# Compact 64x64 tiles in the second mixer's triangular inverse, and normalisation per half of the tokens

## What is computed

```python
def rmsnorm(x, g):
    xf = x.astype(jnp.float32)
    y = xf * lax.rsqrt(jnp.mean(xf * xf, axis=-1, keepdims=True) + EPS)
    return (y * g.astype(jnp.float32)).astype(x.dtype)
```

```python
    def step(S, inp):
        r_t, k_t, v_t, d_t, kk_t, a_t = inp
        S = (S * d_t[:, :, None, :]
             - jnp.einsum('bhvk,bhk->bhv', S, kk_t)[..., None] * (kk_t * a_t)[:, :, None, :]
             + v_t[..., None] * k_t[:, :, None, :])
        return S, jnp.einsum('bhvk,bhk->bhv', S, r_t)
```

## Time and profile before

| | us |
|---|---|
| median of three runs (range) | 2458.49 (2456.34 to 2458.69) |
| the profiled execution | 2457.47 |
| its span, first to last instruction | 2455.7 |
| PE busy in the span | 2189.4 (89%) |
| DVE busy | 656.2 (27%) |
| ACT busy | 355.1 (14%) |
| POOL busy | 136.7 (6%) |

### The profile page before, as it was taken

One profiled execution on the slowest core, in us unless ns is written; L12 is line 12 of the kernel. 1 busy time (PEld: TensorE's weight loads), 2 busy tenths in 40 slices (PEclk: granted clock), 3 DMA queues, 4 the chain that ended last, 5 costly groups with the idle time before them and its releaser, 6 DMA issues. The chain is left out here.

```text
span 2455.7 us, 32351 instructions
## 1 busy us (share of the span) xinstructions
PE 2189.4 (89%) x13312; PEld 1917.6 (78%) x13312; DVE 656.2 (27%) x1048; ACT 355.1 (14%) x658; POOL 136.7 (6%) x136
## 2 busy tenths in 40 slices
PE   6997889877899999999899867939999999999687
PEld 5876777746788888887688645739999999999676
DVE  4286332353200000003531376131001100000033
ACT  1552111110000000001222111010111100111011
POOL 0011111141000000000000200010000000000100
PEclk9998877878999999999999866959999999999888
DMA  7211000011122222212222210028777778877520
GB/s 302 69 52 43 1 1 1 1 35 48 60 78 77 69 79 93 72 65 67 87 73 77 75 52 20 18 77 290 238 258 254 254 250 284 269 239 250 212 81 35
DMA packets 70963, 282.78 MB, mean 115 GB/s; under 512 B 7952, under 2 KB 9104, under 8 KB 69600
## 3 DMA queue, kind: packets, MB, share of 16 engines
q1 hardware_dynamic: 63680, 255.53, 31.3%
q0 software_dynamic: 5040, 19.02, 2.0%
q10 hardware_dynamic: 2160, 7.03, 0.8%
HBM read 255.46 MB, written 26.10 MB: 115 GB/s over the span
## 5 line engine op out<-in xcount | busy, mean ns | idle before, releaser
L189 PE MATMUL ps<-normed,ring 128*128 128x260 f32 (+1 forms) x3424 | 764.1, 385 | 16.7 <-DVE normed L232 16.7
L189 PEld LDWEIGHTS ps<-normed,ring 128*128 128x128 f32 (+1 forms) x3424 | 652.4, 191 | 125.6 <-issue 22.9
L2140 PE MATMUL ps<-proj,ring 128*128 128x144 f32 x3168 | 392.7, 287 | 5.3 <-issue 4.8
L2140 PEld LDWEIGHTS ps<-proj,ring 128*128 128x128 f32 x3168 | 390.8, 191 | 7.6 <-issue 7.0
L2150 PE MATMUL ps<-wide,ring 128*128 128x144 f32 x1584 | 210.9, 293 | 0.0
L2150 PEld LDWEIGHTS ps<-wide,ring 128*128 128x128 f32 x1584 | 205.2, 196 | 0.9
L189 PE MATMUL ps<-proj,ring 128*128 128x260 f32 x640 | 151.8, 399 | 18.3 <-PEq L877 8.4
L189 PEld LDWEIGHTS ps<-proj,ring 128*128 128x128 f32 x640 | 127.2, 200 | 41.0 <-issue 14.0
L189 PE MATMUL ps<-wide,ring 128*128 128x260 f32 x704 | 154.6, 383 | 0.9 <-DVE wide L1176 0.9
L189 PEld LDWEIGHTS ps<-wide,ring 128*128 128x128 f32 x704 | 133.7, 190 | 21.8 <-DVE wide L1176 1.3
L2216 DVE TENSOR_TENSOR wide<-temps,ps 128x144 f32<-128x144 f32 x99 | 30.1, 304 | 369.7 <-PE ps L2140 369.7
(11 more groups left out here) (441 smaller groups left out, 1860.0 us busy)
## 6 DMA issues: line engine op xcount, KB each, us to landing
ring<-in_w_moe_gu SPq DMA_DIRECT2D x198, 512.0 KB, 4.3
ring<-in_w_moe_dn SPq DMA_DIRECT2D x72, 704.0 KB, 5.7
ring<-in_w_gu SPq DMA_DIRECT2D x44, 512.0 KB, 3.6
ring<-in_w_in_cd SPq DMA_DIRECT2D x25, 512.0 KB, 3.5
ring<-in_w_in_ab SPq DMA_DIRECT2D x22, 512.0 KB, 3.6
ring<-in_w_dn SPq DMA_DIRECT2D x16, 704.0 KB, 4.1
ring<-in_w_ple SPq DMA_DIRECT2D x16, 640.0 KB, 3.9
slots_hbm<-wide POOLq DMA_DIRECT2D x1, 9216.0 KB, 30.1
```

The source lines that it names most:

```text
L189: mm = pe.matmul(dst[0:width, a:a + HALF], slab[:, k * width:(k + 1) * width], x[:, a:a + HALF], start=first and k == 0, stop=last and k = ...
L2140: mm = pe.matmul(hid_psum(m, s), slot(Q_MOE + 2 * m + s)[:, f * P:(f + 1) * P], XG(f), start=f == 0, stop=f == KD - 1)
```

## The change

The head pairs are stored compactly: AL, DD, EE, GG, OO become 128x512 (8 tiles of 64 columns, head 0 on the upper, head 1 on the lower partitions), and each 128x128 product of the loop becomes two 64x64 products, one for each head, on its own quarter of PE's array (`hs`, `hp`). PSUM halves are 256 columns (`hp4`). EE starts from a second set of products, with the operands of ab exchanged, masked with `upper`, in place of the transposes L704 and the ACT copy L782. The masks shrink from 961 to 641 columns; a POOL memset of the block-diagonal tiles falls away. In the normalisation, `norm_dve` does reciprocal and scaling first for columns 0 to 259, then for 260 to 519; the first slab does all eight k for the first half and then all eight for the second (`first_product`); the router waits again before its third token group; the output's stores wait for the second half of their tiles.

```diff
@@ -226,18 +226,22 @@
 
         def norm_dve(dve, gain):
             dve.wait_ge(norm_root.sem, norm_root.at(1))
-            dve_step.on(dve.reciprocal(RINV, ROOT))
-            dve.wait_ge(dve_step.sem, dve_step.count)
-            for k in range(KD):
-                u_ready.on(dve.scalar_tensor_tensor(out=u3[:, k, :], in0=h3[:, k, :], scalar=v(gain, k), in1=RINV,
-                                                    op0=ALU.mult, op1=ALU.mult))
-
-        def normed(pe):
-
-            def tile(k):
-                pe.wait_ge(u_ready.sem, u_ready.at(k + 1))
-                return u3[:, k, :]
-            return tile
+            for a in (0, HALF):
+                half = slice(a, a + HALF)
+                dve_step.on(dve.reciprocal(RINV[:, half], ROOT[:, half]))
+                dve.wait_ge(dve_step.sem, dve_step.count)
+                for k in range(KD):
+                    u_ready.on(dve.scalar_tensor_tensor(out=u3[:, k, half], in0=h3[:, k, half], scalar=v(gain, k),
+                                                        in1=RINV[:, half], op0=ALU.mult, op1=ALU.mult))
+
+        def first_product(pe, dst, slab, width=P):
+
+            for n, a in enumerate((0, HALF)):
+                for k in range(KD):
+                    pe.wait_ge(u_ready.sem, u_ready.at(KD * n + k + 1))
+                    mm = pe.matmul(dst[0:width, a:a + HALF], slab[:, k * width:(k + 1) * width],
+                                   u3[:, k, a:a + HALF], start=k == 0, stop=k == KD - 1)
+            return mm
...
-        rwmask, level = Dm[:, 0:P], lambda l: Dm[:, P * (1 + l):P * (2 + l)]
-        sign, i64 = Dm[:, 7 * P:7 * P + 1], Dm[:, 7 * P + 1:7 * P + 65]
+        rwmask, level = Dm[:, 0:P], lambda l: Dm[:, P + 64 * l:P + 64 * (l + 1)]
+        upper, sign, i64 = Dm[:, 512:576], Dm[:, 576:577], Dm[:, 577:641]
         pairs = lambda ap: ap.rearrange("p (n c) -> p n c", c=P)
-        AL, DD, EE, GG = [pairs(u_sb[:, n * 1024:(n + 1) * 1024]) for n in range(4)]
-        OO = pairs(C[:, 0:1024])
+        heads = lambda ap: ap.rearrange("p (n c) -> p n c", c=64)
+        AL, DD, EE, GG, EO = [heads(u_sb[:, n * 512:(n + 1) * 512]) for n in range(5)]
+        OO = heads(C[:, 0:512])
...
+        def hp(bank, hh, n):
+
+            j = 512 * (n // 4) + 64 * (n % 4)
+            return ps[bank][64 * hh:64 * hh + 64, j:j + 64]
+
+        def hs(tile, hh, n):
+
+            return tile[64 * hh:64 * hh + 64, n, :]
+
+        def hp4(bank, cc):
+
+            return heads(ps[bank][:, 512 * cc:512 * cc + 256])
...
-                    for cc in range(2):
-                        for t in range(4):
-                            n = (4 * cc + t) * P
-                            for hh in range(2):
-                                mm = pe.matmul(ps[0][64 * hh:64 * hh + 64, n + 64 * hh:n + 64 * hh + 64],
-                                               rk(t, 2 * s + cc, RKAP, hh), rk(t, 2 * s + cc, RB, hh),
-                                               start=True, stop=True)
-                    g["ab_mm"].on(mm)
+                    for first, second, at in ((RKAP, RB, 0), (RB, RKAP, 512)):
+                        for cc in range(2):
+                            for t in range(4):
+                                n = at + 64 * (4 * cc + t)
+                                for hh in range(2):
+                                    mm = pe.matmul(ps[0][64 * hh:64 * hh + 64, n:n + 64], rk(t, 2 * s + cc, first, hh),
+                                                   rk(t, 2 * s + cc, second, hh), start=True, stop=True)
+                        g["ab_mm"].on(mm)
...
-                    w(pe, "d_ready", s + 1)
                     w(pe, "am_read", 2 * s + 2)
-                    for n in range(8):
-                        mm = pe.transpose(ps[1][:, n * P:(n + 1) * P], DD[:, n, :], ident)
-                    g["e_mm"].on(mm)
                     w(pe, "v_read", s + 1)
                     for l in range(5):
                         for cc in range(2):
                             if l == 0:
-                                w(pe, "o_ready", 2 * s + cc + 1)
-                                w(pe, "e_read", s + 1)
+                                w(pe, "o_ready", s + 1)
                             else:
                                 w(pe, "next_o", 8 * s + 2 * (l - 1) + cc + 1)
                                 w(pe, "de_read", nth(s, l - 1, cc))
                             for n in range(4 * cc, 4 * cc + 4):
-                                mm = pe.matmul(ps[0][:, n * P:(n + 1) * P], OO[:, n, :], EE[:, n, :], start=True, stop=True)
+                                for hh in range(2):
+                                    mm = pe.matmul(hp(0, hh, n), hs(OO, hh, n), hs(EE, hh, n), start=True, stop=True)
                             g["g_mm"].on(mm)
                         for cc in range(2):
                             w(pe, "g_read", nth(s, l, cc))
                             for n in range(4 * cc, 4 * cc + 4):
-                                if l < 4:
-                                    pe.matmul(ps[1][:, n * P:(n + 1) * P], GG[:, n, :], DD[:, n, :], start=True, stop=True)
-                                mm = pe.matmul(ps[2][:, n * P:(n + 1) * P], DD[:, n, :], GG[:, n, :], start=True, stop=True)
+                                for hh in range(2):
+                                    if l < 4:
+                                        pe.matmul(hp(1, hh, n), hs(GG, hh, n), hs(DD, hh, n), start=True, stop=True)
+                                    mm = pe.matmul(hp(2, hh, n), hs(DD, hh, n), hs(GG, hh, n), start=True, stop=True)
                             g["eg_mm"].on(mm)
...
-                    w(act, "e_mm", s + 1)
-                    g["e_read"].on(act.activation(u_sb[:, 2048:3072], ps[1][:, :], ACT.Copy))
...
-                            g["g_read"].on(act.activation(u_sb[:, 3072 + 512 * cc:3584 + 512 * cc],
-                                                          ps[0][:, 512 * cc:512 * cc + 512], ACT.Copy))
+                            g["g_read"].on(act.activation(GG[:, 4 * cc:4 * cc + 4], hp4(0, cc), ACT.Copy))
...
-                    w(dve, "ab_mm", s + 1)
-                    for hh in range(2):
-                        j = 64 * hh
-                        S(dve.tensor_copy(AL[j:j + 64, :, j:j + 64], pairs(ps[0][j:j + 64, :])[:, :, j:j + 64]),
-                          g["ab_read"] if hh else None)
+                    w(dve, "ab_mm", 2 * s + 1)
+                    S(dve.tensor_copy(AL, heads(ps[0][:, 0:512])))
+                    w(dve, "ab_mm", 2 * s + 2)
+                    S(dve.tensor_copy(EO, heads(ps[0][:, 512:1024])), g["ab_read"])
                     S(dve.tensor_tensor(OO, AL, spread(level(0), 8, 1), ALU.mult))
-                    S(dve.tensor_tensor(DD, spread(ident, 8, 1), OO, ALU.subtract), g["d_ready"])
-                    for cc in range(2):
-                        n = slice(4 * cc, 4 * cc + 4)
-                        S(dve.tensor_tensor(OO[:, n], AL[:, n], spread(level(1), 4, 1), ALU.mult), g["o_ready"])
+                    S(dve.tensor_tensor(DD, spread(i64, 8, 1), OO, ALU.subtract))
+                    S(dve.tensor_tensor(EO, EO, spread(upper, 8, 1), ALU.mult))
+                    S(dve.tensor_tensor(EE, spread(i64, 8, 1), EO, ALU.subtract))
+                    S(dve.tensor_tensor(OO, AL, spread(level(1), 8, 1), ALU.mult), g["o_ready"])
...
-                            n, half = slice(4 * cc, 4 * cc + 4), slice(512 * cc, 512 * cc + 512)
+                            n = slice(4 * cc, 4 * cc + 4)
                             w(dve, "eg_mm", nth(s, l, cc))
                             if l < 4:
-                                S(dve.tensor_tensor(DD[:, n], DD[:, n], pairs(ps[1][:, half]), ALU.subtract))
-                            S(dve.tensor_tensor(EE[:, n], EE[:, n], pairs(ps[2][:, half]), ALU.subtract), g["de_read"])
+                                S(dve.tensor_tensor(DD[:, n], DD[:, n], hp4(1, cc), ALU.subtract))
+                            S(dve.tensor_tensor(EE[:, n], EE[:, n], hp4(2, cc), ALU.subtract), g["de_read"])
...
@@ -1127,8 +1137,11 @@
...
-                            product(pe, pt(2 * (m % 2) + s), slot(Q_GU + 2 * m + s), KD,
-                                    normed(pe) if m == 0 and s == 0 else lambda n: u3[:, n, :]).then_inc(slab_used.sem, 1)
+                            if m == 0 and s == 0:
+                                mm = first_product(pe, pt(0), slot(Q_GU))
+                            else:
+                                mm = product(pe, pt(2 * (m % 2) + s), slot(Q_GU + 2 * m + s), KD, lambda n: u3[:, n, :])
+                            mm.then_inc(slab_used.sem, 1)
...
@@ -1936,8 +1949,8 @@
...
-                        if tt == 0:
-                            pe.wait_ge(u_ready.sem, u_ready.at(k + 1))
+                        if tt in (0, 2):
+                            pe.wait_ge(u_ready.sem, u_ready.at(KD * (tt // 2) + k + 1))
...
@@ -2259,7 +2272,7 @@
...
```

(22 more changed lines are left out.)

3 lines of the change are left out of this document (1 added, 2 removed).

## The result

| | us |
|---|---|
| before, median of the runs beside it | 2458.59 |
| after, median of four runs (range) | 2386.84 (2383.67 to 2390.46) |
| ratio, 95% interval | 0.9709 (0.9691 to 0.9727) |
| the profiled execution after, its span | 2388.85, 2387.0 |

The gain is 71.8 us; the forecast had 56.3, and 2386.8 lies just under the lower end of its range, 2388. The direction and the mechanism held, sizes did not. Where the 15.5 us came from is the question of what follows.

A forecast was written before the change was run, and what follows sets the result against it. Bound: a single chain through PE, with DVE's subtractions limiting between loop levels. Loops 43.9, heads 9.9, chain -2 and normalisation 4.5 make 56.3 us less: 2402 us; range 2390 to 2418, 8 in 10 within 2388 to 2436.

The forecast's parts named there:

- The bound: Recurrence: a single chain through PE; in the loop PE limits 4.58 us of a 6.36 us level, DVE 1.78.
- DVE's gap: Loop, between levels: DVE's two subtractions delay the next g; the 1.78 us become 1.24.
- The loop: Loop of the inverse, four sets: a level takes 4.04 us instead of 6.36, a loop 21.1; 43.9 us less.
- the record's price at the high clock: Loop's 64-column products on PE: 0.035 us each, taken from L764, bounds 0.029 and 0.045.
- The heads: Stretches before the loops: 2.2 us less in each of three sets, 3.3 in the first; together 9.9 less.
- The chain: Chain over the two chunks, instructions unchanged: 2 us lost in all to an earlier clock fall, between 0 and 8.
- The normalisation: Reciprocal and scaling in halves, at all places: 4.5 us less, between 5.6 less and 3.2 more.
- The output: Last normalisation, with no product to hide the split under: the end moves 1.9 to 3.2 us later, 3.0 taken.
- The second embedding: Gated embeddings, both: PE comes to the slab from other products without a pause, so nothing gained.
- (b): Rival: products don't overlap in the loop, 0.057 us each, a level 5.8; 20 us less in all, 2438; chance 0.12.
- (a): Rival: the clock stays low in the loop, a level 6.04 us; 19 us less in all, 2439; chance 0.13.
- (c): Rival: each change of quarter in the loop costs 0.13 us a record, so slower, about 2538; chance 0.04.

The follow-up runs named there:

- E first: Changed kernel with DVE's two subtractions of each half in the loop swapped, E before D, PE waiting for D: 2377.9 us, 0.9671 of the kernel before.
- heads apart: Changed kernel, each loop group making all products of the first head, then those of the second, instead of in turn: 2467.2 us, 1.0033 of the kernel before.
- inverse alone: Changed kernel with the normalisation of before, one reciprocal and eight scalings over all columns: 2400.7 us, 0.9752 of the kernel before.
- normalisation alone: Kernel before with only the normalisation's part of the change, in halves, and nothing of the inverse: 2450.4 us, 0.9962 of the kernel before.

## Why the prediction was right and wrong

**The bound: right.** PE and DVE's gap limit the loop as read from the earlier trace rows, and the change took from both. The run with E first shows the gap's half, the run with the heads apart PE's.

**The loop: mis-sized, 6.6 us.** The step of the prediction that failed is the record's price at the high clock, 0.035; it is 0.0295. The 0.035 came from a group of sixteen measured up to the next group's start. That group, L764, is followed by a change of shape, from 128*64 to 64*64, so its 0.56 us hold the price of that change. Eighty records in a row do not pay it. The better row was at hand: at the low clock the prediction had 0.06 in turn for 0.236 of 128 columns, about a quarter, and a quarter of 0.1145 is 0.0286. It stood there as a bound and not as the value. Step by step in the second set: first level up to the end of its products 4.5 us (forecast 5.2), three levels of 3.70 (4.04), the last 3.8 (3.8); 19.4 instead of 21.1. In the first level the clock helped too: 0.91 over 19.38 us means 3.5 us of low clock, where 4.5 were taken. DVE's gap was 0.10 too short in the forecast, which hid part of the error.

**The heads: nearly right.** 11.3 less, forecast 9.9. They take 10.3 to 10.7 us, forecast 10.8 to 11.1. The added products and DVE's wait for them cost what was put down for them, within 0.6 us a set.

**The chain: the sign of a small term.** The forecast had 2 us lost, because a loop less dense would hand over a clock that falls earlier. The later three chains are 29.4 to 30.3 us, before 29.7; together they lost 0.6 us. The first is 14.3 instead of 16.9 in the profile, and 14.0 in the run with E first, but 16.5 and 16.6 in two other runs with the same chain. Of the 4.1 us between forecast and profile, some 2.6 are therefore where the clock fell in this execution, and luck; why it falls 12.3 us after the chain's start in one run and 7.9 us after it in another is left open.

**The normalisation: mis-sized, 3.6 us, and not at its front.** Alone it gave 8.1, forecast 4.5, bounds 5.6 less to 3.2 more, and the upper bound failed too. PE's starts were right (2.45 us for 2.4). The step that failed is that each start is worth its 1.9 us. Until the clock rises the work goes half as fast, so an earlier start alone is worth half of itself, and an earlier rise gives the other half. In the feed-forward part (1.9 + 2.9) / 2 makes 2.4 us, and DVE's first operation behind the products does come 2.4 us earlier after the reciprocal's start (654.42 - 633.58 = 20.84 before, 590.44 - 572.02 = 18.42 after). In layer 1 (1.9 + 0.4) / 2 makes 1.15, and ACT's first copy of the second slab comes 1.15 us earlier (1211.48 - 1191.09 = 20.39 before, 1146.22 - 1126.98 = 19.24 after). In layer 0 it was 0.7, as the clock rose 0.6 us later, and in the router 2.2, so that its bound of 2 failed too. Together these four are 6.4 us where the forecast had 7.5: less, not more.

The rest of the 3.3 to 3.8 us that the table gives for the feed-forward part, layer 1 and the router comes far behind the normalisation, in code that the change does not touch. The largest piece that a row shows is in layer 1: the same sixteen records, some 270 us after the reciprocal, fall at the low clock before the change and at the high one after it, and are 1.7 us shorter.

```profile
1460.01 3.65 PE L1706 MATMUL ps<-consts,proj 128*128 128x128 f32 x16 [1.39 <-PEq L1519]
```

```profile
1395.12 1.94 PE L1719 MATMUL ps<-consts,proj 128*128 128x128 f32 x16 [1.40 <-PEq L1532]
```

In the inverse alone they take 3.65 us, in the normalisation alone 1.94, so here it goes with the split. The output was right: 2.7 later for 3.0. The second embedding was right within 0.2 us, the first lost 0.7.

**What the sum left out.** The block behind the recurrence, whose code is the same, moved between 124.8 and 129.6 us over the profiles of this study. The forecast took everything behind the recurrence to move along unchanged. With this the 15.5 us are accounted for: 6.6 in the loops, 4.1 in the chains, 1.4 in the heads, 5.0 in the stretches between the norms (9.5 for 4.5), less the 4.8 that this block gave back, and the 3.1 between medians and traces. A spread of 5 us belonged into the range for this; the changed kernel's own runs lie 6.8 apart (2383.7 to 2390.5).

**The rivals.** (b) fell for this order: the products overlap. The heads apart are what it described, and they cost more than it said, because the low clock of (a) came with them. (c) fell for the loop: there the quarter changes with every product, and a record takes 0.0295 all the same. But the row from which it took its price, 0.13 a record in the chain, shows a real cost in its own place: 0.147 us for each change of shape, which the chain pays over and over. The prediction read the row as a threat to the change and not as a gain left lying; the 68.2 us that the grouped chain gives are nearly as much as the change itself.

**The range.** Most of the way to its lower end came from the record's lower bound, 0.029, which is what was measured. The terms that were too small (loop, heads, chain, normalisation) all leaned to the same side, and the range had nothing for the clock in code that the change does not touch.

## What to carry to other kernels

Here products on 64x64 quarters paid about a quarter of a full product's time only where neighbours in PE's order lay on different quarters; sorted by quarter, the loop took 37.6 us where the full products had taken 31.9, with the clock at 0.50 instead of 0.93. Sort small products by shape, and put those that go to different quarters next to each other: a change of shape cost 0.147 us here, more than four overlapped records. Price a small product from a long run of its like, and where a stretch runs at the low clock, ask what the edit does to the moment when the clock rises, not only to the work.

## What the runs showed of the hardware

- Two 64x64 products on different quarters, in one PSUM bank and on different partitions, overlap: 0.0295 us a record in turn at the high clock; neighbours on one quarter take 0.107 each at the low one, where ab in turn pays 0.06.
- A change between products of 64 rows and of 128 rows costs 0.147 us at the high clock. A group between two changes takes 0.26 us with two records and with four, 0.37 with eight, 0.61 with sixteen.
- The clock did not follow PE's busy share. With the heads apart PE was busy 36.4 of 37.6 us at a clock of 0.50; in turn 16.8 of 19.4 at 0.91. In the chain it was busy 29.4 of 30.0 at 0.54 with shapes in turn, and 9.0 of 9.9 at 1.00 with shapes grouped. In both pairs the products are the same and the order that lets products overlap has the high clock.
- Where the clock changes fall moves untouched code: the same block took 124.8 to 129.6 us, the same chain 14.0 to 16.6, the same sixteen records of layer 1 3.65 or 1.94.
- Work that starts at the low clock gains half of an earlier start and half of an earlier rise: 2.4 us for 1.9 and 2.9, 1.15 for 1.9 and 0.4.
